# Mixture-of-experts decoder layer on one core: the gate copy, the first gathers and the matmuls on zeros in another order

## What is computed

```python
scores = jax.nn.sigmoid((t @ router_w).astype(jnp.float32))
...
gate = jnp.sum(jax.nn.one_hot(top_idx, N_EXPERTS, dtype=jnp.float32) * top_w[..., None], axis=1)
...
for e in range(N_EXPERTS):
    h = jax.nn.silu(t @ w1[e]) * (t @ w3[e])
    y = y + gate[:, e:e + 1] * (h @ w2[e])
```

## Time and profile before

| | |
|---|---|
| median of 3 runs | 1003.58 us (1003.42 to 1004.42) |
| the profiled execution, its own time | 1003.6 us |
| its span | 1002.0 us |
| mean granted clock of TensorE | 0.979 of full speed |
| busy: PE, DVE, ACT, POOL | 914.1, 627.2, 479.2, 254.5 us |
| chain that ended last | PE 55%, DVE 15%, issue 13%, POOL 8% |
| expert blocks | 550.75 us (block 0) to 949.23 us (start of block 15) |
| from the start of block 15 to the end of the span | 52.8 us |

### The profile page before, as it was taken

How to read it: one execution, slowest core, us unless ns; L and a number is a source line. 1 busy time by engine, 2 the same in 40 slices (tenths; PEclk the granted TensorE clock), 3 DMA queues, 4 the chain that set the end, 5 groups by cost and what they waited for, 6 DMA issues and landing times.

```text
span 1002.0 us, 16808 instructions
## 1 busy us (share of the span) xinstructions
PE 914.1 (91%) x6255; PEld 702.4 (70%) x6255; DVE 627.2 (63%) x833; ACT 479.2 (48%) x756; POOL 254.5 (25%) x250
## 2 busy tenths in 40 slices
PE   8999999999999999899998899989888988998980
PEld 6778998886777777678885676666666666666660
DVE  3202824665646746776558996866666666677986
ACT  3312522235655645732226164655555555555874
POOL 3000000000000000040000775744444444644234
PEclk9999999999999999999999999999999999999995
DMA  9301120002001301187322799898888888998974
GB/s 259 62 22 43 45 61 22 1 2 62 22 22 43 75 1 43 43 300 297 127 105 89 203 290 346 265 293 276 293 284 286 277 279 291 303 296 286 323 248 158
DMA packets 102139, 168.89 MB, mean 169 GB/s; under 512 B 24949, under 2 KB 48685, under 8 KB 102080
## 3 DMA queue, kind: packets, MB, share of 16 engines
q1 hardware_dynamic: 88720, 143.74, 41.8%
q0 software_dynamic: 10320, 23.18, 10.4%
q10 hardware_dynamic: 3040, 1.19, 0.5%
HBM read 143.81 MB, written 24.54 MB: 168 GB/s over the span
## 4 chain that ended last, share of the span: by engine, by line
PE 55%; DVE 15%; issue 13%; POOL 8%; ACT 5%; DMA 3%; DVEq 0%; SPq 0%; POOLq 0%; ACTq 0%
PE bank L896 11%; PE bank L898 11%; PE bank L897 11%; DVE el L2012 8%; POOL xg L764 4%; PE pz L1012 3%; PE bank L1090 2%; PE pz L896 2%; PE pz L897 2%; PE pz L898 2%; PE bank L1106 2%; POOL xg L761 1%; ACT eh L1601 1%; POOL slot_tokens L688 1%; PE pz L1250 1%
## 5 line engine op out<-in xcount | busy, mean ns | idle before, releaser
L2012 DVE TENSOR_TENSOR el<-er,eh 128x1024 fp32r<-128x1024 f32 x192 | 223.8, 1220 | 94.4 <-ACT eh L1601 94.4
L1601 ACT ACTIVATE eh<-er 128x1024 fp32r<-128x1024 f32 x192 | 189.9, 1053 | 7.7 <-PE pz L898 7.7
L896 PE MATMUL pz<-eh,xh 128*128 128x512 f32 x256 | 104.4, 408 | 16.1 <-DVE el L2012 14.0
L1943 DVE TENSOR_TENSOR_SCAN Qs<-Qs,own 128x128 f32<-128x128 f32 (+7 forms) x48 | 65.0, 1355 | 69.7 <-ACT Qs L1488 69.7
L896 PE MATMUL bank<-xT_hi,w_hi 128*128 128x512 f32 (+1 forms) x264 | 106.1, 402 | 1.9 <-DVE xT_lo L1828 1.9
L635 POOL MEMSET rw<- 128x128 f32 x1 | 0.2, 205 | 415.2 <-DVE mix L1936 415.2
L898 PE MATMUL bank<-xT_hi,w_lo 128*128 128x512 f32 (+1 forms) x264 | 102.4, 388 | 0.0
L897 PE MATMUL bank<-xT_lo,w_hi 128*128 128x512 f32 (+1 forms) x264 | 101.8, 386 | 0.0
L897 PE MATMUL pz<-el,xh 128*128 128x512 f32 x256 | 100.0, 391 | 0.0
L898 PE MATMUL pz<-eh,xl 128*128 128x512 f32 x256 | 99.8, 390 | 0.0
L896 PEld LDWEIGHTS pz<-eh,xh 128*128 128x128 f32 x256 | 48.1, 188 | 36.4 <-DVE el L2012 18.7
(11 more groups left out here) (358 smaller groups left out, 1825.3 us busy)
## 6 DMA issues: line engine op xcount, KB each, us to landing
er<-in_w_dram SPq DMA_DIRECT2D x192, 512.0 KB, 5.6
w_raw<-in_w_in_dram SPq DMA_DIRECT2D x21, 512.0 KB, 3.8
x_row<-in_x_dram SPq DMA_DIRECT2D x8, 512.0 KB, 9.0
xres<-in_x_dram SPq DMA_DIRECT2D x8, 512.0 KB, 5.6
sum_scratch<-x SPq DMA_DIRECT2D x8, 512.0 KB, 3.9
x_scratch<-x1p SPq DMA_DIRECT2D x8, 512.0 KB, 2.6
cx<-sum_scratch SPq DMA_DIRECT2D x8, 512.0 KB, 7.9
out_dram<-cx SPq DMA_DIRECT2D x5, 512.0 KB, 3.0
```

Of the source, the lines that this page charges most:

```text
L896: pe.matmul(dst, lh, rh, start=(k == k_first), stop=False)
L1601: act.activation(eh[:, p, :], er[:, p, :], ACT.Copy).then_inc(S["eh_ok"], 1)
L1943: dve.tensor_tensor_scan(Qs[:, h, 0:W][:, ::-1], Qs[:, h, 0:W][:, ::-1], own1[:, T - W:][:, ::-1], 0.0, ALU.mult, ALU.max).then_inc(S["sca ...
L2012: dve.tensor_tensor(el[:, p, :], er[:, p, :], eh[:, p, :].bitcast(F32), ALU.subtract).then_inc(S["el_ok"], 1)
```

## The change

1. **Gates.** In `step`, `gates` of block b - 2 stands ahead of `quarters`, `gather` and `load_table` of block b; it stood behind them. The same in the unrolled first three steps with a table gate.
2. **`add_first(0)`** stands behind the load of expert 3's table; it stood ahead of it and of the wait for the scatters.
3. **Own semaphore for the first rows.** The gather of expert 0's whole rows counts on `sg_in`, no longer on `xg_in`. GpSimd's wait for it ahead of `first_gather(1)` is gone; all later counts are adapted.
4. **PE's opening.** Twelve matmuls on zeros more between two small groups of expert 0, four more in expert 1's, seven in place of six; `spread_slots(1)` stands ahead of the first half of block 0's `spare_gu`.
5. **DVE's opening.** `quarter_rows(1)` stands eleven instructions earlier; piece 2 of block 0 is split behind `x_lo` and no longer ahead of it.

```diff
             first_gather(0)
             pool.wait_ge(S["xgB_in"], 16)
-            pool.wait_ge(S["xg_in"], 16)
             first_gather(1)
             scatter(0)
...
-            add_first(0)
             for c in range(2):
                 pool.wait_ge(S[f"idl_st{c}"], 16 * (NT + 1 - c))
...
             def step(r, b, ahead=True):
+                gates((r + 2) % 4, b - 2)
                 quarters(r, b)
                 gather(r, b)
                 if ahead:
                     load_table((r + 1) % 4, b + 1)
-                gates((r + 2) % 4, b - 2)
                 add_rows((r + 2) % 4, b - 2)
...
                     load_table(3, 3)
+                    add_first(0)
                     quarters(3, 3)
...
                     for u in range(4):
+                        if u:
+                            gates((u + 2) % 4, 2 + u)
                         quarters(u, 4 + u)
                         gather(u, 4 + u)
                         load_table((u + 1) % 4, 5 + u)
                         if u:
-                            gates((u + 2) % 4, 2 + u)
                             add_rows((u + 2) % 4, 2 + u)
...
+                if b < 2:
+                    spin((12, 4)[b], (None, po[:, 0:GLA_W])[b])
                 pe.wait_ge(S["oneh_ok"], n + 2)
...
             slot_tokens(0)
-            spin(6)
+            spin(7)
...
                 if first_block(b):
-                    spare_gu(b, range(0, 2))
                     pe.wait_ge(S["selm_ok"], 3 * NQ + 2)
                     spread_slots(1)
+                    spare_gu(b, range(0, 2))
                     first_transposes()
...
             slot_masks(1)
             piece_lo(0, 1)
+            quarter_rows(1)
...
-            quarter_rows(1)
-
...
             row_gates(0)
-            piece_lo(0, 2)
...
-                    for p in range(3, AHEAD):
+                    for p in range(2, AHEAD):
                         piece_lo(b0, p)
```

More of the change, by code:

```diff
@@ L702, in first_gather @@
                 if b == 0:
-                    pool.indirect_dma_start(xgAs[0][:, :], None, sum_dram, bass.IndirectOffsetOnAxis(firstA[:, 0:1], 0)).then_inc(S["xg_in"], 16)
+                    pool.indirect_dma_start(xgAs[0][:, :], None, sum_dram, bass.IndirectOffsetOnAxis(firstA[:, 0:1], 0)).then_inc(S["sg_in"], 16)
                 for c in range(NB - 1) if b else ():
@@ L715, in _ @@
             pool.wait_ge(S["xgB_in"], 32)
-            pool.wait_ge(S["xg_in"], 16 * NB)
+            pool.wait_ge(S["xg_in"], 16 * (NB - 1))
             first_gather(2)
@@ L758, in gather @@
                 pool.wait_ge(S["xgB_in"], 16 * b)
-                pool.wait_ge(S["xg_in"], 16 * (NB - 1) * b - 16 * (NB - 2))
+                pool.wait_ge(S["xg_in"], 16 * (NB - 1) * (b - 1))
                 pool.sem_inc(S["pool_go"], 1)
@@ L1232, in first_transposes @@
             def first_transposes():
-                pe.wait_ge(S["xg_in"], 16)
+                pe.wait_ge(S["sg_in"], 16)
                 for k in range(NK):
@@ L2021, in rows_turn @@
             def rows_turn(b, buf):
-                dve.wait_ge(S["xg_in"], 16 * (NB - 1) * b + 16)
+                dve.wait_ge(S["xg_in"], 16 * (NB - 1) * b)
                 dve.wait_ge(S["piece_done"], (NPIECE - 1) * (b - 1) + 2 * NF)
@@ L2210, in spare_sums @@
             def spare_sums(b):
-                dve.wait_ge(S["sg_in"], 32)
+                dve.wait_ge(S["sg_in"], 48)
                 dve.wait_ge(S["raw_done"], NPIECE * b + NPIECE)
```

## The result

The changed kernel takes 964.77 us as a median of four runs (963.63 to 966.87), the kernel before 1003.50 (1002.54 to 1004.42) beside it. The ratio is 0.9617, with a 95% interval of 0.9598 to 0.9635: 38.7 us less. The forecast was 962.2 with a range of 957 to 974. The profiled execution took 964.94 us with a span of 963.3.

A forecast was written before the change was run, and what follows sets the result against it. The prediction took ACT's wait for GpSimd's gate copy, queued behind a gather, to hold PE's pitch at 26.59 us. It summed 38.0 (gates) + 2.8 (expert 3) + 0.6 (opening) = 41.4 us off 1003.6: 962.2 us, range 957 to 974.

The forecast's parts named there:

- The gates: Blocks 4 to 15: early gate copies free ACT's yB, so 11 pitches fall to the free one, saving 38.0 us.
- free pitch: Distance between block starts with no table gate waited for, from block 3 to 4: 23.13 us, against 26.59 in the loop.
- The slack of the loop: Loop: gathers land 9.7 us after a block's start, 5.9 to spare; adds land 13 after, PE suffers from 23.4.
- Rival (b): Loop: adds land later than 23.4 us after a block's start, pitch 25, about 983 us; chance 0.05.
- Rival (a): Loop: DMA engines become the bound, pitch 23.3 to 24.3, 969.5 us (965 to 975); chance 0.22.
- The gather of expert 3: Blocks 2 to 3: gather 2.4 us earlier, PE's wait 1.8 shorter, with 1.0 from the clock 2.8 us saved.
- the table: Before block 3: expert 3's table, loaded ahead of the adds, lands 1.3 us sooner, between 0 and 4.8.
- The 0.5 for the scatters: Before expert 3's table: scatters land 0.5 us sooner with the adds queued later.
- the 0.6 from part 5: The opening's 0.6 us, reaching the second round of scatters and so expert 3's gather.
- For the clock I took half of the 1.9: Behind the wait for hTl before block 3: half of 1.9 us lost to low clock is saved, counted as 1.0.
- The opening: Parts 3 to 5, block 0: PE's first product 1.8 us earlier, but DVE limits the gain to 0.6 us (0 to 1.8).
- The tail: From block 15's start to the end, 52.8 us: 0 us saved.

The follow-up runs named there:

- e1: The kernel before with the move of the gate copies alone (part 1); 975.24 us, ratio 0.9616.
- e2: The changed kernel with the gate copies put back behind the gathers and table loads; 1007.82 us, ratio 0.9934.
- e3: The changed kernel with the gate copy between the gathers and the load of the next table; 992.92 us, ratio 0.9791.
- e4: The changed kernel with one extra 512 KB DRAM-to-DRAM copy per expert, read by nobody; 969.58 us, ratio 0.9565.
- e11: The changed kernel with four extra 512 KB DRAM-to-DRAM copies per expert, read by nobody; 1013.13 us, ratio 0.9998.
- a2: The changed kernel run again unaltered, on another chip; 965.61 us, ratio 0.9627 against the kernel before.
- e6: The changed kernel with fourteen matmuls on zeros ahead of PE's wait for hTl in block 2; 963.14 us, ratio 0.9614.
- e10: The changed kernel with e6's zeros, e7's scatter rounds, and the adds of expert 1 ahead of expert 4's table; 968.25 us, ratio 0.9547.
- e7: The changed kernel with two of the eight second scatter rounds ahead of expert 2's whole-row gathers; 962.39 us, ratio 0.9594.
- e8: The changed kernel with the adds of expert 0 back ahead of expert 3's table (part 2 undone); 971.28 us, ratio 0.9579.
- e9: The kernel before with parts 1 and 2 of the change, keeping the old opening; 975.86 us, ratio 0.9611.
- e5: The changed kernel with ten matmuls on zeros ahead of PE's first wait for hB; 963.80 us, ratio 0.9602.

## Why the prediction was right, point by point

**The gates: 38.0 predicted, 38.5 measured.** The mechanism and its size held, alone (e1, 39.0 us) and by its absence (e2). The free pitch was 23.09 and not 23.13, which over 11 blocks is the missing half microsecond. The copy costs 1.66 us in its new place, where I had 1.61 from the row of block 14, and it comes out of GpSimd's wait. The Trainium skill, "GPSIMD Engine Reference", section "Key points", has GpSimd contend with DVE instructions that have two SBUF inputs. e3 agrees from the other side: DVE stands idle from 683.05 to 689.58 us there, and the same copy takes 0.20.

**The slack of the loop.** The issue of the last of the five gathers begins at 683.86, that is 4.1 us after block 5's start at 679.74; in the kernel before it was 1.2 after (684.73 against 683.48). Their issue takes 1.58 us as a mean of 52 (line 762, page of after), and did 1.00 before. I had missed that, but had reckoned from 3.7, the end of the table loads behind the gathers, while a landing counts from the start of its issue. So with the 5.96 of landing it is 10.1 against the 15.6 at which DVE asks, 5.5 to spare for my 5.9: two errors that nearly cancel. The adds of the block before were off by more. I had them landed 13 us after a block's start; their issue begins 9.2 us after it (665.88 against 656.65), and they take 9.2 more (the issues of DMAs from block 4 to 15; median us from issue to landing):

```profile
sum_scratch<-yA,tab POOLq DMA_INDIRECT x11, 9.2
```

That is 18.4 us after the start, with ACT's `yB` at 18.9 and the point from which PE suffers at 23.4. Rival (b), to which I gave 0.05, was 5 us away and not 10.

**Rival (a), 0.22.** It did not happen, and e4 shows how far off it was: 352 to 358 GB/s at the same pitch. The argument for it, a busy share of 1.0, was the weak one. The trace has 1.01 and 1.05 at the same pitch of 23.09, so that share doesn't tell when the engines are the bound; the moved bytes do (e11). The Trainium skill ("DMA: Bandwidth & Descriptors", "Where 436 GB/s comes from") gives about 358 GB/s as the limit of HBM for a core. The measurements don't bear that out as the bound here. A copy from DRAM to DRAM both reads and writes HBM (e4's page has 8.39 MB more read and 8.39 MB more written than after's), so I estimate HBM traffic of 352 + 23 = 375 GB/s in e4, at no cost, and of 372 + 80 = 452 in e11.

**The gather of expert 3: 2.8 predicted, 1.1 measured in one trace and -0.5 in the other (block 2 to 4: 52.15 before, 51.04 in after, 52.65 in a2).** From the start of the lead-in (at 542.56 us before, 542.91 in after, 542.48 in a2), which leaves out how block 1 has moved, the last gather goes out after 77.8 us before (620.32), 76.0 in after (618.90) and 76.1 in a2: 1.8 and 1.7 us earlier, where I had worked out 2.4. All of it is the table, which landed in 6.13 in place of 7.89 (chain of after; 5.81 in a2), 1.8 to 2.1 sooner where I took 1.3. The 0.5 for the scatters and the 0.6 from part 5 didn't come: the table is asked for 0.3 to 0.4 us later than before. Chain of after:

```profile
604.21 6.13 DMA tab<-slot_tokens
...
623.64 5.37 DMA sum_scratch<-yA,addA
```

PE's wait (timeline of after, the answer to the earlier trace rows) is 1.55 shorter, and in a2 (3.44) 0.57; I had 1.8:

```profile
627.60 1.21 PE L1350 MATMUL bank<-eh,hTl 128*128 128x512 f32 x4 [2.46 <-DVE hTl L2326]
```

Two steps failed. *For the clock I took half of the 1.9*: nothing was saved. Stretches from the end of that wait to block 3, of before, after, a2 and e6:

```profile
628.17:633.64 5.47, 5.47 (x17) 4.06 (x17) 2.66 (x3) 1.41 (x2) 3.55 (x3) 0.69 0.77 170
627.60:633.09 5.49, 5.49 (x17) 4.06 (x17) 2.66 (x3) 1.41 (x2) 3.45 (x4) 0.69 1.07 299
626.98:633.52 6.54, 6.54 (x17) 4.94 (x17) 2.65 (x3) 2.04 (x4) 4.50 (x5) 0.56 1.05 308
624.61:628.48 3.87, 3.87 (x16) 2.92 (x17) 2.65 (x3) 1.41 (x2) 2.45 (x2) 1.00 1.08 288
```

In before and after the first four matmuls take 1.2 us and the clock is down only behind them; in a2 it is down at once (2.08 us), and the same work takes 1.05 us longer. Only zeros in the wait (e6, e10) kept it up. *The next wait was missing*: block 3 now takes 23.56 in after and not 23.13, since `yB` of expert 2 runs at 633.82, 0.73 after the block's start, held by the adds of expert 1. These were issued at 623.64 and landed 10.1 us later (DMA issues of after, 621 to 630 us):

```profile
sum_scratch<-yA,addA POOLq DMA_INDIRECT x1, 10.1
```

The 5.37 us in the chain above is only the piece up to the moment at which ACT began to wait. In a2 `yB` runs 0.6 us ahead of block 3, which takes 23.13. e6 shows this wait growing as the first one goes (2.1 us behind block 3's start); in e10 `yB` of expert 2 is early again and that of expert 3 is late. I had asked what is late next for the loop and not for these first blocks.

**The opening: 0.6 predicted, -0.6 in one trace, 0.55 in the other.** As told, the clock is 1.00 from 547.0 to 554.5 (0.54 before), `spare_gu` takes 1.93 us for 32 matmuls and the first product starts at 558.28, by the lead-in 1.6 us earlier, where I had 1.8. DVE is then the engine that all meet at `hB`, as I had it: PE stands 1.65 us there where it stood 0.60. In after the clock fell behind that wait, in a2 it didn't:

```profile
566.78 0.33 PE L1327 MATMUL pz<-ident,hB 128*128 128x128 f32 x1 [1.65 <-DVE hB L2304]
...
568.04 0.63 PE L897 MATMUL pz<-el,xh 128*128 128x512 f32 x1
```

```profile
566.34 0.33 PE L1327 MATMUL pz<-ident,hB 128*128 128x128 f32 x1 [1.67 <-DVE hB L2304]
...
568.58 0.39 PE L896 MATMUL pz<-eh,xh 128*128 128x512 f32 x1
```

My range of 0 to 1.8 had left out a loss, and after shows one: behind a wait that was made longer the clock can fall, though at this place it did so in one of the four traces with that wait (after, a2, e6, e7).

**The two terms were no sum.** This is the error of form. In after block 1 starts 1.2 us later into the lead-in than in a2, but its wait for `hTl` is 1.0 shorter (2.46 against 3.44), and PE goes on behind it 84.7 and 84.5 us into the lead-in, 0.9 and 1.1 earlier than before. What was left of that went in a2 to the clock and in after to `yB`; block 4 starts at 656.65 in both. Expert 3's rows come by a chain of GpSimd and DMA that PE's start of block 1 hardly moves; what PE gains in the opening it waits longer at `hTl`. I had added 0.6 for the opening to the 2.8. The lead-in says what both brought: 114.21 - 113.74 = 0.5 us and 114.21 - 114.17 = 0.0, for 3.4 predicted. Hence 964.8 and not 962.2. On the chips where PE stops in the tiny matmuls block 1 starts 3.7 us sooner with the new opening, and there e2 shows 6.4 us for parts 2 to 5. Part 2 alone, as e8 against e2 to e4, is 1.9 us of block 1 to 4 with the new opening (after and a2, one kernel, differ by 1.6 in that column). With the old one (e9 against e1) block 3 starts 1.6 us sooner into the lead-in, 99.0 against 100.6, but then lasts 25.03 us against 23.09, as `yB` comes 2.1 us after its start: the next wait takes it all.

**The tail: 0 predicted.** 963.3 - 910.61 = 52.7 us, 52.8 before.

## What to carry to other kernels

An instruction that needs nothing its neighbours wait for should stand ahead of their wait in an in-order queue, even where it runs several times slower: 0.26 us of work in the wrong place cost 38.5. Judge by the pitch, with one block that is free of the wait as the yardstick, since idle time on another engine doesn't say what the loop pays. And don't add gains of steps that meet at one join: take the latest arrival, then ask for the arrival behind it.

## What the runs showed of the hardware

- GpSimd issues gathers slower when DVE has no gaps beside it: 1.58 us a piece as a mean of 52, in single rows 0.95 or about 1.9, where the mean was 1.00.
- The clock fell behind a wait of PE of 1.65 us and stayed up behind one of 1.67 us at the same place in another execution of the same kernel. Of 14 waits of 1.58 to 2.03 us for `xl` and `hB` in the opening it fell behind four (after 1.65, e10 1.89, e1 and e9 2.02), and stayed up behind ten, the longest of all (2.03, before) among them. Behind the wait for `hTl` ahead of block 3, 2.46 to 4.35 us in the 12 traces that have it, it always fell; fourteen matmuls on zeros in the wait held it up (e6, e10). Against e6 the fall cost 1.6 us from that wait to block 3 where it came behind four matmuls (before, after), 2.7 where it came at once (a2).
- On two of the chips PE stops in groups of tiny matmuls for about 0.5 us at a time, with nothing in the profile that it waits for. The kernel before is 11 us slower on them.
- Accumulating adds of whole rows to DRAM land 9.1 to 9.8 us after their issue (median 9.2) beside transfers of 330 GB/s in all, and 10.1 us for the one issued at 623.64.
- A small table that is loaded behind two such adds lands in 7.9 to 9.0 us (before, e8, e1), and ahead of them in 5.8 to 6.8 (after, a2, e2 to e5, e7, e9).
- A busy share of 1.05 of the DMA engines at 352 GB/s did no harm; with the same share at 372 GB/s PE waited for weights.
